# A ring of eight row buffers instead of two in a backward state scan, and a new order of its first loads

## What is computed

```
# the SSD scan, run on the reversed sequence for the backward direction
states = einsum('bcjgn,bcjgrp->bcgrpn', b_mat, xdt * to_end[..., None])   # one state per chunk
h_next = h * chunk_decay + states[chunk]                                  # carried from chunk to chunk
# the modulation, one row of 6 * 1024 numbers per sequence
mod = silu(c) @ w_ada + b_ada
```

## Time and profile before

| | |
|---|---|
| Time, median of 3 runs | 3703.0 us (3700.46 to 3708.77) |
| The profiled execution, its own time | 3708.0 us |
| Its span, first to last instruction | 3706.2 us |
| PE busy in the span | 3153.6 us (85%) |
| DMA in the span | 437.62 MB, mean 118 GB/s |
| The stage `scan_back`: SP's first load to DVE's last add | 802.33 to 913.78 us |
| The next stage's first load | 915.26 us |

### The profile page before, as it was taken

How to read it: one execution, slowest core, us unless ns; L and a number is a source line. 1 busy time by engine, 2 the same in 40 slices (tenths; PEclk the granted TensorE clock), 3 DMA queues, 4 the chain that set the end, 5 groups by cost and what they waited for, 6 DMA issues and landing times. The chain is left out here.

```text
span 3706.2 us, 33835 instructions
## 1 busy us (share of the span) xinstructions
PE 3153.6 (85%) x10424; PEld 1648.4 (44%) x10425; DVE 1432.8 (39%) x2033; ACT 540.3 (15%) x1058; POOL 1210.2 (33%) x1202
## 2 busy tenths in 40 slices
PE   7999999956787467759999928999999999999940
PEld 3555555532555344525555523444444444444420
DVE  2835423413788545513333361222122221222238
ACT  1112222211232100011111101101101101011012
POOL 0116766712666300002222202223222232222329
PEclk9999999977989777879999969999999999999975
DMA  5122232235222364262222124344454354442235
GB/s 238 74 76 80 99 118 94 82 137 211 66 82 89 94 183 145 77 239 91 97 97 91 53 119 151 102 136 125 130 163 126 113 154 152 117 121 45 56 95 206
DMA packets 131695, 437.62 MB, mean 118 GB/s; under 512 B 16884, under 2 KB 45300, under 8 KB 122644
## 3 DMA queue, kind: packets, MB, share of 16 engines
q1 hardware_dynamic: 86488, 291.18, 22.5%
q0 software_dynamic: 24752, 81.35, 9.2%
q10 hardware_dynamic: 20368, 63.94, 4.5%
HBM read 300.03 MB, written 136.38 MB: 118 GB/s over the span
## 5 line engine op out<-in xcount | busy, mean ns | idle before, releaser
L2008 PE MATMUL bank<-wg,exp_ht 128*128 x1008 | 455.0, 594 | 15.4 <-DVE exp_ht L2091 15.4
L2026 PE MATMUL bank<-wd,exp_hid_t 128*128 x1008 | 442.9, 592 | 0.9 <-ACT exp_hid_t L2062 0.9
L2008 PE MATMUL bank<-wu,exp_ht 128*128 x1008 | 442.9, 592 | 0.0
L1967 POOL DMA_INDIRECT x<-exp_out,exp_rows x63 | 102.6, 1629 | 870.0 <-DVE exp_out L2112 826.1
L2112 DVE TENSOR_TENSOR exp_out<-bank,exp_gates 128x512 f32<-128x512 f32 x126 | 81.2, 686 | 778.1 <-PE bank L2026 778.1
L1550 PE MATMUL bank<-mix_wo,mix_yt 128*128 128x512 f32 x768 | 342.4, 600 | 19.0 <-issue 11.5
L571 PE MATMUL bank<-x_t,w_in 128*128 128x512 f32 x768 | 336.0, 596 | 5.4 <-DVE x_t L481 5.4
L571 PE MATMUL bank<-w_in,x_t 128*128 128x264 f32 (+1 forms) x1152 | 339.6, 455 | 0.0
L2026 PEld LDWEIGHTS bank<-wd,exp_hid_t 128*128 128x128 f32 x1008 | 191.4, 190 | 241.6 <-issue 241.6
L2008 PEld LDWEIGHTS bank<-wu,exp_ht 128*128 128x128 f32 x1008 | 191.5, 190 | 241.1 <-issue 241.1
L2008 PEld LDWEIGHTS bank<-wg,exp_ht 128*128 128x128 f32 x1008 | 188.0, 192 | 227.5 <-issue 227.5
(11 more groups left out here) (350 smaller groups left out, 3830.2 us busy)
## 6 DMA issues: line engine op xcount, KB each, us to landing
wg<-in_w_gate SPq DMA_DIRECT2D x16, 2048.0 KB, 7.9
wu<-in_w_up SPq DMA_DIRECT2D x16, 2048.0 KB, 9.2
wd<-in_w_down SPq DMA_DIRECT2D x16, 2048.0 KB, 9.2
x_t<-in_x_t SPq DMA_DIRECT2D x6, 2048.0 KB, 9.2
mix_xt<-in_x SPq DMA_DIRECT2D x6, 2048.0 KB
x<-mix_v ACTq DMA_DIRECT2D x24, 512.0 KB, 2.6
h<-mix_h ACTq DMA_DIRECT2D x24, 512.0 KB, 2.7
com_v<-x SPq DMA_DIRECT2D x24, 512.0 KB, 3.9
```

What stands on the lines that cost most here:

```text
L1967: pool.indirect_dma_start(out=y_dram, out_offset=bass.IndirectOffsetOnAxis(ap=rows[:, j:j + 1], axis=0), in_=out[:, j, :], in_offset=None, ...
L2008: mul = pe.matmul(bank[:, :], ht[:, j, k, :], flat(of[:, bass.ds(e % 2, 1), k * DE:(k + 1) * DE]), start=k == 0, stop=k == KT - 1)
L2026: mul = pe.matmul(bank[:, :], hid_t[:, j, k, :], flat(wd[:, bass.ds(e % 2, 1), k * D + q * WIDE:k * D + (q + 1) * WIDE]), start=k == 0, st ...
```

## The change

`rows` gets eight buffers, and each its own semaphore. Row n now goes into buffer n % 8, and SP asks for it when the states of row n - 8 are counted. The first eight rows need no wait: rows 0 and 1 are asked for as before, rows 2 to 7 behind piece 0 of the weights and ahead of pieces 1 and 2. POOL and PE read the buffers by the new number. `xw` and the weight ring stay as they were.

```diff
+    RING = 8
-        rows = sb("rows", [P, 2, SSD + 2 * STATE])
+        rows = sb("rows", [P, RING, SSD + 2 * STATE])
-        rows_here = [S(f"rows_here{j}") for j in range(2)]
+        rows_here = [S(f"rows_here{j}") for j in range(RING)]
...
                 def load(n):
-                    sp.dma_start(rows[:, n % 2, :], xb[chunk_of(n) * P:(chunk_of(n) + 1) * P, :]).then_inc(rows_here[n % 2], 16)
+                    sp.dma_start(rows[:, n % RING, :], xb[chunk_of(n) * P:(chunk_of(n) + 1) * P, :]).then_inc(rows_here[n % RING], 16)
                 load(0)
                 load(1)
                 sp.dma_start(bias[:], b_mod).then_inc(b_here, 16)
-                for s in range(SLOTS):
+                sp.dma_start(wt[:, 0], w_mod[0]).then_inc(w_here[0], 16)
+                for n in range(2, RING):
+                    load(n)
+                for s in range(1, SLOTS):
                     sp.dma_start(wt[:, s], w_mod[s]).then_inc(w_here[s], 16)
-                for n in range(2, NT):
-                    sp.wait_ge(states, n - 1)
+                for n in range(RING, NT):
+                    sp.wait_ge(states, n - RING + 1)
                     load(n)
...
-                    pool.wait_ge(rows_here[j], n // 2 * 16 + 16)
+                    pool.wait_ge(rows_here[n % RING], n // RING * 16 + 16)
```

More of the change, by code:

```diff
@@ L828, in _ @@
                     c = chunk_of(n)
-                    pool.wait_ge(rows_here[j], n // 2 * 16 + 16)
+                    pool.wait_ge(rows_here[n % RING], n // RING * 16 + 16)
                     if n >= 2:
                         pool.wait_ge(states, n - 1)
-                    pool.tensor_tensor(by_head(xw[:, j, :]), by_head(rows[:, j, 0:SSD]),
+                    pool.tensor_tensor(by_head(xw[:, j, :]), by_head(rows[:, n % RING, 0:SSD]),
                                        wide(C.dt_to_end[:, c:c + 1, back]), ALU.mult).then_inc(weighted, 1)
@@ L860, in _ @@
                     for g in range(2):
-                        mul = pe.matmul(C.bank[j][:, g * 256:(g + 1) * 256], rows[:, j, SSD + g * STATE:SSD + (g + 1) * STATE],
+                        mul = pe.matmul(C.bank[j][:, g * 256:(g + 1) * 256], rows[:, n % RING, SSD + g * STATE:SSD + (g + 1) * STATE],
                                         xw[:, j, g * 256:(g + 1) * 256], start=True, stop=True)
```

## The result

The changed kernel takes 3676.2 us (median of 4 runs, 3671.0 to 3678.8) against 3704.7 us, a ratio of 0.9921 (95% interval 0.9904 to 0.9939). Two more comparisons, on the chips of the later experiments, gave 0.9904 (0.9889 to 0.9918) and 0.9925 (0.9912 to 0.9939). The forecast was 3681 us with a range from 3669 to 3693, and the measured time lies in it; the gain is 28.5 us where 22 were forecast. The ratios leave out two executions, one of the kernel before (5026.7 us) and one of the order alone (5491.2 us), whose clock was 0.64 and 0.58 on average where the others had 0.92 to 0.93.

The account below looks back on a forecast made before the run. No engine fills the stage; POOL waits for rows, PE for POOL, DVE for PE. 15.8 us by sums(7) + 8.5 tail - 0.23 semaphores = 24, with mutual waiting 22: from 3703.0 to 3681 us, range 3669 to 3693.

Parts of the forecast that it names:

- Rows 2 to 7 first: Stage start: row 2 lands right behind piece 0, so sums(0) starts at about 817 against 827.28, 10 us won.
- the queue out of order: Rival: SP's queue not serving in issue order, rows 2 to 7 landing among pieces 1 and 2; 3691 us, chance 0.03.
- What the rows push back: First units: six rows delay pieces 1 and 2 by 7.5 us; row 8 may land at 842, sums(3) at 844.
- The units: Sums(3) to sums(7): four units of 7.9 us each, PE and DMA level, sums(7) at 875.6, 15.8 us won by then.
- mutual waiting: Last four units: level servers wait for each other, 0.5 us taken for each, bringing 24 us down to 22.
- The tail: From sums(7) to the last add's end: 13.9 us instead of 22.4, rows at DVE's 1.44 us each, gain 8.5 us.
- Semaphores and SP: Six more semaphores cleared between two meetings cost 0.23 us; SP's 12 transfers issued in a row cost nothing.
- The starved rows: Rival: each piece lets only one row past, lead used up by mid-stage; 12 us less gain, 3693 us, chance 0.14.
- sign of being wrong: Among the signs on the stage's timelines: holes on POOL ending with a row load beyond row 8, meaning rows starve.
- The rival of a faster PE: PE holds full clock, units go at the DMA's pace, row 8 not late; gain about 29 us, 3674 us, chance 0.11.
- a floor only: Whole stage: 24 rows at 1.25 us and 8 pieces at 4.9 make 69.2 us, the floor of the DMA.
- Half clock in the whole stage: Rival: PE stays at 1.2 GHz, units cost 11.9 us, 7 us slower, about 3710 us, chance 0.04.

Follow-up runs that it names:

- the order alone: Against the changed kernel: two buffers, rows 2 and 3 between pieces 0 and 1, each when its buffer is free; stage 105.4 us, ratio 0.9985.
- the ring alone: Against the changed kernel: eight buffers kept, but pieces 0, 1, 2 asked for before rows 2 to 7; stage 83.1 and 82.9 us, ratio 0.9925 and 0.9934.

## Why the prediction was right, and where it was not

**Rows 2 to 7 first, 10 us.** sums(0) starts 15.2 us into the stage; 14.7 were forecast (817 less 802.33). The step itself was right. As a term of the gain it was not: the ring alone, without it, has the same stage within the spread (82.9 and 83.1 us against 78.8 to 85.3). The 10 us are given back at pieces and rows that come later, because the early start of PE meets DMA engines that are full up to 853. The prediction had priced the change without these 10 us, in the rival of the queue out of order: a gain of 12 us, 3691. The ring alone measured that case, and gained 25.6 and 29.5 us in two comparisons. So the sum follows the changed kernel's time line, but it gives the order 10 us that the ring brings without it. For the ring alone the same prices gave less than half of what was measured. That the total lies in the range is in part luck.

**What the rows push back.** Forecast, counted from the start of the stage: piece 2 at 33.3 at the latest, row 8 at 39.7, sums(3) at 41.7. Measured: sums(2), which waits for piece 2, at 31.0, row 8 on POOL at 36.9, sums(3) at 39.1, with the hole on PE in front of sums(2) and none of size at row 8. Right in kind, 2 to 3 us too late.

**The units.** This is the step that was mis-sized. Four units were put at 7.9 us, with half a microsecond of mutual waiting each; from sums(3) at 838.54 to sums(7) at 867.61 they took 29.1 us, 7.3 each, 4.5 us less in all. A piece beside rows costs 4.96 us and not 5.4, and a row beside pieces about 1.0 and not 1.25, so the DMA's price of a unit is about 7.0 us and not 7.9. The 5.4 came from slow records: in the kernel before 67 of the 621 records of 16 KB between 834 and 880 took over 0.7 us (median 0.61), in the changed kernel 1 of 596 between 826 and 858; why is not shown. PE's mean clock was 0.89 to 1.00 in the stretches from 821 on, not 0.76. The three units from sums(0) to sums(3) took 23.9 us where 27 were forecast, by piece 2 and row 8 as above. In the stage's gain, then, the start of sums(0) is 0.5 us short of the forecast, these three units give 3.1 us more, the last four 4.5 more, the tail 0.7 less and the semaphores 0.2 less: 28.4 us in place of 22.1, up to rounding.

**The tail.** 13.9 us forecast, 14.6 measured, at 1.52 us a row and not 1.44. It is safe in every version with four or eight buffers, and makes 7.8 of the 28.8 us.

**Semaphores and SP.** 0.23 us forecast for six clears, 0.4 us measured between the stages; one execution of each kernel is too little to tell. SP took 3.75 us to issue rows 2 to 7, where one row alone takes 0.33; the engines had a share of 0.97 meanwhile, so putting that at nothing held.

**The rivals.** The starved rows are real: 5.9 us apart, one for each piece. They are also the prediction's own sign of being wrong, holes on POOL behind row 8 that end with a row load. They cost PE one hole of 3.25 us in the changed kernel (5.5 us in two holes at rows 9 and 10 in its third execution), not 12 us, because seven rows were in hand when it began. The rival of a faster PE came closest: 29 us and 3674 against 28.5 and 3676.2 measured, and the clock did rise, to 0.94 from sums(3) to sums(7). But PE still waited for piece 2 and for rows, and the four units stayed 0.3 us each above the DMA's price, so its mechanism is there only in part. That the DMA engines are the bound, which I had as a floor only, is what the order's 10 us ran into: without pieces 3 to 7 the stage is 10 us shorter. The page "DMA: Bandwidth & Descriptors" of the Trainium skill, section "Queues, rings and completion order", lets the engines take turns between queues, with a packet of typically 9 to 17 descriptors from one queue before the next. The turns agree with the rows 5.9 and 3.46 us apart; the unit does not, since here the queue changes after nearly every descriptor. The 7.7 us of the earlier trace rows, which the prediction read as agreeing with such packets, do not decide it: that load stood behind another row's, issued at 833.0 and not yet landed. Beside that very piece, from 837.0 to 838.6, a record of 16 KB begins at the end of all 33 records of 3 KB. Half clock in the whole stage did not come: its mean was 0.86.

## What to carry to other kernels

Price the stage's transfers as a whole before pricing any one wait. In this stage their sum was near the time that was left: a load that moved forward made another late, and the deeper buffer, which filled pauses of the DMA, gave the time. Here the engines changed queues after nearly every descriptor, so a small load got past a large one only once per transfer as long as both had 128 descriptors; smaller descriptors for the large one let the rows past sooner (3.46 us apart, not 5.9). A ring for the small loads must hold, when the large ones begin, as many as will be missing over their whole run. And a term that is right at its own place (here sums(0), 10 us earlier) is not yet a term of the gain: follow it to the end of the stage.

## What the runs showed that was not expected

Mixed transfers on two queues did not slow each other: from 826 to 858 the changed kernel's DMA engines were full with 417 GB/s, near the 431 GB/s of pieces alone. And the same kernel's stage took 78.8, 82.7 and 85.3 us in three executions: where three small holes depend on which transfer has its turn, a single profile is not enough to rank two versions that differ by less than some 6 us.
